# The third block's four engines: instruction order by sort keys, replaced by an order written out step by step

## The reference, cut to what matters

```python
def hybrid_layer(x, norm_gain, w_in, ...):
    hn = rms_norm_3(x, norm_gain)
    proj = jnp.einsum('btd,de->bte', hn, w_in)      # 30 column groups of 128, and 4 forget columns
    log_f = jax.nn.log_sigmoid((ff + b_forget).astype(jnp.float32)).transpose(0, 2, 1)
    o_fox = forgetting_attention(rms_norm_3(fq), rms_norm_3(fk), fv, log_f)
    o_moba = moba_attention(rms_norm_3(mq), rms_norm_3(mk), mv, rel_bias...)
    o_sb = stick_breaking_attention(sq, sk, sv)     # no softmax: logs, a scan, an exponential
    o_swa = swa_sink_attention(rms_norm_3(wq), rms_norm_3(wk), wv, sinks, rel_bias...)
    y = concatenate([o_fox * silu(fg), o_moba * silu(mg), o_sb * silu(sg), o_swa * silu(wg)])
    return x + jnp.einsum('bte,ed->btd', y, w_out)
```

## Time and profile before

| what | value |
|---|---|
| median of 3 runs | 3691.18 us (3691.16 to 3693.05) |
| the profiled execution | 3688.29 us, its span 3686.5 us |
| PE busy in the span | 3161.8 us (86%) |
| DVE busy, ACT busy | 2409.5 us (65%), 1398.1 us (38%) |
| third block | from about 3157 us of the span to its end |

### The profile page before, as it was taken

The page is one execution under the profiler, slowest core; times in us unless marked ns, Lnnn a source line. Parts: engine busy times, 40 slices in busy tenths (PEclk is TensorE's granted clock), DMA queues, the critical chain, the costliest instruction groups (busy, mean ns, idle before and its releaser), DMA issues. The chain is left out here.

```text
span 3686.5 us, 34649 instructions
## 1 busy us (share of the span) xinstructions
PE 3161.8 (86%) x11816; PEld 2026.5 (55%) x11816; DVE 2409.5 (65%) x4718; ACT 1398.1 (38%) x2337; POOL 698.0 (19%) x583
## 2 busy tenths in 40 slices
PE   8988799987887787777788999985999999498878
PEld 4655544433333333333366877764788888465556
DVE  4876456676776777677476445654788888644444
ACT  2324312222222222222253333432788888534442
POOL 0000023344444444444200000000122221000000
PEclk9998799999899999998998999997999999799888
DMA  8322189999999999999821222234899999421101
GB/s 278 113 86 82 40 306 393 404 404 421 417 419 415 415 414 416 420 410 413 317 75 52 78 69 72 86 109 185 291 370 379 372 366 372 147 58 46 29 29 58
DMA packets 351924, 905.63 MB, mean 246 GB/s; under 512 B 29953, under 2 KB 170753, under 8 KB 285570
## 3 DMA queue, kind: packets, MB, share of 16 engines
q0 software_dynamic: 84000, 549.52, 36.4%
q1 hardware_dynamic: 267746, 353.85, 28.1%
HBM read 896.45 MB, written 31.99 MB: 252 GB/s over the span
## 5 line engine op out<-in xcount | busy, mean ns | idle before, releaser
L258 PE MATMUL peer_acc<-peer_uv,peer_diag 128*128 128x512 f32 x2048 | 998.3, 640 | 235.5 <-ACT peer_diag L314 232.5
L435 DVE CUSTOM_DVE_ANT_0 peer_uv<-peer_uv,firsts_h 128x1024 f32<-128x1024 f32 x512 | 627.6, 1227 | 347.2 <-DMA peer_uv<-in_peer_uv,peer_experts 345.7
L258 PEld LDWEIGHTS peer_acc<-peer_uv,peer_diag 128*128 128x128 f32 x2048 | 408.7, 204 | 806.6 <-issue 487.3
L210 POOL DMA_INDIRECT peer_uv<-in_peer_uv,peer_experts x512 | 574.0, 1121 | 1225.0 <-PE peer_acc L258 714.9
L3056 DVE TENSOR_TENSOR slotted_low<-slotted_raw,slotted_high 128x2048 fp32r<-128x2048 f32 x192 | 434.1, 2288 | 66.8 <-ACT slotted_high L3005 66.8
L3005 ACT ACTIVATE slotted_high<-slotted_raw 128x2048 fp32r<-128x2048 f32 x192 | 365.5, 1920 | 64.4 <-PE slotted_h L2962 51.8
L314 ACT ACTIVATE peer_diag<-all_consts,peer_weights 128x128 f32<-128x128 f32 x512 | 166.0, 391 | 329.2 <-DVE peer_weights L428 300.8
L305 ACT ACTIVATE peer_act_in<-peer_act_in 128x4 f32<-128x4 f32 (+1 forms) x130 | 26.6, 205 | 612.2 <-DVE peer_act_in L435 612.2
L2962 PE MATMUL slotted_h<-slotted_high,slotted_xT_high 128*128 128x512 f32 x512 | 205.3, 401 | 6.2 <-DVE slotted_low L3056 4.1
L2962 PE MATMUL slotted_h<-slotted_high,slotted_xT_low 128*128 128x512 f32 x512 | 201.8, 394 | 0.0
L2962 PE MATMUL slotted_h<-slotted_low,slotted_xT_high 128*128 128x512 f32 x512 | 201.8, 394 | 0.0
(11 more groups left out here) (751 smaller groups left out, 5766.5 us busy)
## 6 DMA issues: line engine op xcount, KB each, us to landing
slotted_raw<-in_moe_w SPq DMA_DIRECT2D x192, 1024.0 KB, 8.4
mixers_raw<-in_w_in SPq DMA_DIRECT2D x56, 512.0 KB, 3.7
firsts_ada_raw<-in_w_ada SPq DMA_DIRECT2D x64, 256.0 KB, 2.7
third_raw<-in_w_in SPq DMA_DIRECT2D x30, 512.0 KB, 3.6
firsts_raw<-in_w_in SPq DMA_DIRECT2D x28, 512.0 KB, 4.4
firsts_ada_first<-in_w_ada SPq DMA_DIRECT2D x8, 1024.0 KB, 13.3
peer_uv<-in_peer_uv,peer_experts POOLq DMA_INDIRECT x512, 10.9
ffn_w_raw<-in_peer_wq SPq DMA_DIRECT2D x10, 512.0 KB, 21.9
```

The source lines that it names most:

```text
L210: pool.indirect_dma_start(uv[:, n % R, :, :].rearrange("p a d -> p (a d)"), None, A["peer_uv"], bass.IndirectOffsetOnAxis(ap=experts[:, si ...
L258: mm = nc.tensor.matmul(acc[t % 2][j][:, :], diag[:, n % 4, :], uv[:, n % R, 1, j * BANK:(j + 1) * BANK], start=(m == 0), stop=(m == E - 1))
L435: nc.vector.tensor_tensor_reduce(uv[:, n % R, 0, :], uv[:, n % R, 0, :], h2[:, t, :], 1.0, 0.0, ALU.mult, ALU.add, act_in[:, side, i:i + 1 ...
```

## The change: what it does

Nothing is computed otherwise, and no buffer, bank or semaphore is added or removed. Four things are changed in how the lists are written.

1. `weave` is replaced in the third block by `weave_by`. It takes a string in which each letter names a generator (a is the first argument, b the second, and so on) and a number says how often it goes on. The due times no longer play a part between generators.
2. The generators of the softmax works sort their own steps with a spacing of 2.9 for all kinds. With it the list of each engine has S of work n+1 ahead of T of work n throughout. Before, this was so for moba and swa only, while in fox a work ended (M) before the next began (S).
3. Pieces can be interrupted after every 3 matmuls of the input product (one k), not only after 12. The closing product has such places after every 3 as well, and the string does not use them.
4. On DVE the five operations of a stick head can be interrupted in three places.

```diff
+def weave_by(order, *programs):
+
+    for program in programs:
+        next(program, None)
+    for part in order.split():
+        for _ in range(int(part[1:] or 1)):
+            next(programs[ord(part[0]) - ord("a")], None)
+    assert all(next(program, None) is None for program in programs)
...
                     for k in range(KD):
-                        if k == 4:
-                            yield (starts[p] + ends[p]) / 2
+                        if k:
+                            yield starts[p] + (ends[p] - starts[p]) * k / KD
...
             for n in range(n_works):
-                later += [(work_key[n], 0, n), (work_key[n] + 3.0, 1, n), (work_key[n] + 5.0, 2, n)]
+                at = 2.9 * n
+                later += [(at, 0, n), (at + 3.0, 1, n), (at + 5.0, 2, n)]
...
                     chain(nc.vector.scalar_tensor_tensor(s, z, 0.0, l, ALU.max, ALU.add))
+                    yield sb_key(q) + 6.0 + 2.5 * i
...
             def _(pe):
-                weave(rows_tensor(pe), products(pe), spare_tensor(pe), soft_tensor(pe), stick_tensor(pe))
+                weave_by(THIRD_ORDER["tensor"], rows_tensor(pe), products(pe), spare_tensor(pe), soft_tensor(pe), stick_tensor(pe))
...
+THIRD_ORDER = {
...
+    "tensor": (
+        "a8 b9 c b8 c b8 c b8 c b2 c5 b d2 b6 c b8 c5 b5 c b d b d b5 d2 b d b d2 b d b d2 b2 d b d2 b d b d2 b d "
```

More of the change, by code:

```diff
@@ L3507, in products @@
                         for kk in range(2):
+                            if t or kk:
+                                yield starts[p] + (ends[p] - starts[p]) * (2 * t + kk) / KD
                             k = 2 * kp + kk
@@ L3908, in soft_scalar @@
             for n in range(n_works):
-                later += [(work_key[n] + 2.0, 0, n), (work_key[n] + 4.0, 1, n)]
+                at = 2.9 * n
+                later += [(at + 2.0, 0, n), (at + 4.0, 1, n)]
             for key, what, n in sorted(later):
@@ L3926, in soft_vector @@
             for n in range(n_works):
-                later += [(work_key[n] + 1.0, 0, n), (work_key[n] + 6.0, 1, n)]
+                at = 2.9 * n
+                later += [(at + 1.0, 0, n), (at + 6.0, 1, n)]
             for key, what, n in sorted(later):
@@ L4057, in _ @@
             def _(sp_queue):
-                weave(weights_in(sp_queue), loads(sp_queue), rows_out(sp_queue))
+                weave_by(THIRD_ORDER["sync"], weights_in(sp_queue), loads(sp_queue), rows_out(sp_queue))
                 sp_queue.wait_ge(stored, 16 * 2 * NT)
@@ L4062, in _ @@
             def _(pe):
-                weave(rows_tensor(pe), products(pe), spare_tensor(pe), soft_tensor(pe), stick_tensor(pe))
+                weave_by(THIRD_ORDER["tensor"], rows_tensor(pe), products(pe), spare_tensor(pe), soft_tensor(pe), stick_tensor(pe))
             @block.scalar
             def _(act):
-                weave(rows_scalar(act), rounded(act), emptied_by_scalar(act), gates_opened(act), spare_scalar(act),
+                weave_by(THIRD_ORDER["scalar"], rows_scalar(act), rounded(act), emptied_by_scalar(act), gates_opened(act), spare_scalar(act),
                       forget_scalar(act), soft_scalar(act), stick_scalar(act))
@@ L4071, in _ @@
             def _(dve):
-                weave(rows_vector(dve), rests(dve), spare_vector(dve), forget_vector(dve), soft_vector(dve),
+                weave_by(THIRD_ORDER["vector"], rows_vector(dve), rests(dve), spare_vector(dve), forget_vector(dve), soft_vector(dve),
                       stick_vector(dve), rows_closed(dve))
+THIRD_ORDER = {
+    "sync": (
+        "b a3 b a35 c a c7 "),
+    "tensor": (
[6 rows of a table added]
+    "scalar": (
[4 rows of a table added]
+    "vector": (
[4 rows of a table added]
+}
 def constants():
```

## The result

The changed kernel takes **3645.98 us** (median of 4 runs, 3644.53 to 3647.78), beside 3691.17 us of the kernel before in the same session: ratio 0.9878, 95% interval 0.9861 to 0.9896. It is faster by 1.2%. The profiled execution took 3647.78 us, its span is 3646.0 us.

A forecast was written before the change was run, and what follows sets the result against it. PE bounds the middle stage, held up by the fixed order of steps. Work 325, idle 32 and clock 18 make 375 us instead of 419.3, 44 less, so 3646 us as a median; 8-in-10 range 3621 to 3674.

The forecast's parts named there:

- work of PE: Middle stage, PE at full clock: 319 us stay, +1 for a spreading moved in, +5 for changes of kind, together 325.
- place B: Fox norms: PE idle for the reciprocal with six fewer matmuls in front, and at the third spreading; 3.4 us, before 1.
- fox works: E of work 10 1.5 us late behind logarithms and a table load, two more steps late by 0.6; 3 us idle.
- third stick pair: Stick pair of 384 keys: too little PE work covers its activations and DVE operations; short by 3.8 us.
- stick products: Stick products following their transposes at once, 0.3 to 0.6 us in each of 6 pairs, and a turning; 2.5 us.
- place C: Swa norms: PE idle while ACT loads tables, takes the root, stick exponentials and E of work 23; 4.7 us.
- last gate piece: Spreading starts 6.2 us after emptying starts, released by row sums on DVE behind silu and yT; 6.2 us idle.
- small misses: Waits the count does not see, each engine's queue a little late; 4 us, where before some 8.
- clock: Middle stage: time lost to the low clock level, taken as 18 us (bounds 8 and 40) instead of 40 before.
- the 100 us: Middle stage of 419.3 us: the part that is PE idle time and low clock, from which the gain must come.
- the rival of half the gain: Two open works make ACT and DVE queues collide, idle grows by 24 us; 3670 to 3680 us, chance 0.12.
- The clock rival: Many small PE waits raise the low-clock share above 45% (granted clock 0.77 or less), cancelling the gain or slower; chance 0.05.

The follow-up runs named there:

- m_run12: Changed kernel with its written order, but piece matmuls gathered into runs of at least 12: 3673.74 us, ratio 0.9953 to the kernel before.
- x_pipe: Kernel before with only the fox works overlapped, S of the next work ahead of T, by due times: 3689.42 us, ratio 0.9992.
- x_fine: Kernel before with only pieces made interruptible after every 3 matmuls, order still by due times: 3677.02 us, ratio 0.9955.
- c_after: The changed kernel run again unaltered, as companion of later runs: 3647.56 us, ratio 0.9865 to the kernel before.

## Why the prediction was right, point by point

The time came out on the forecast, 3645.98 for 3646, faster as said. The mechanism held in the main, and two terms were mis-sized in opposite directions.

| term of the middle stage | forecast us | measured us |
|---|---|---|
| work of PE | 325 | 323 to 324 |
| place B | 3.4 | 3.0 |
| fox works | 3 | 0.9 |
| third stick pair | 3.8 | 3.3 |
| moba norms | 2.2 | 2.8 |
| stick products | 2.5 | 1.3 |
| place C | 4.7 | 3.9 |
| swa | 2.5 | 1.5 |
| last gate piece | 6.2 | 6.2 |
| small misses | 4 | 0.7 |
| clock | 18 | 23 to 25 |
| sum | 375 | 372.0 |

- **Where the 100 us lay** was right. m_run12 confirms one half of the mechanism, three matmuls that cover C and W. Of the other half it shows that the written order covers E. But the prediction put this down to PE's pattern, and moba and swa had S ahead of T before, with 23.9 us of waits. At the longest of these ACT's own list held E back, and the share of the written lists of ACT and DVE in the gain wasn't measured. x_pipe and x_fine show that neither S ahead of T in fox nor finer places bring it alone.
- **Work of PE**: 6 us more were expected (1 of spreading, 5 of changes of kind), some 4 came. The price goes with the runs, 0.06 and 0.17 us each in the two series. What makes the difference between these two was not measured.
- **Idle time**: 32 expected, 23.6 measured. The long waits were found one by one within 0.8 us. (At place B the row 3257.38 of the earlier trace rows is a weight load. The multiply, L3792, begins at the same time.) What was too large were the allowances for steps that are a little late: fox, swa, stick products and small misses were put at 12 us and took 4.4. The slack of 0.1 to 0.8 us in the pattern was enough, and the rival of half the gain fell with it.
- **Clock**: 18 expected, some 24 measured, and this step failed in its reasoning. I took less than in proportion to the idle time, since most waits would become short and the long ones few. In fact low clock lay at the few long ones, at four places (B and C, the third stick pair with the moba norms, the last gate piece) 51 us in all. The loss was 0.66 us per us of idle time before and about 1.0 after.
- **Place C and the table loads**: root to load, load to exponential follow one another without a gap, 3472.06 to 3472.09 and 3473.37 to 3473.38 in the rows above. The Trainium skill, ScalarE: Activation LUTs, section What ACT_TABLE_LOAD costs, adds a drain of some 1.38 us. The trace disagrees: the wait is 3.90 us, beside the 7.5 us that the drain would have given.
- **The clock rival** had its mechanism right, though not here: in m_run12, 13 waits below 0.7 us in 55 us went with a granted clock of 0.88. The Trainium skill, TensorE: Matmul & The Clock Gate, section A second HAM failure mode, tells of such micro-idles; by this, the trace agrees. In the changed kernel the three-matmul runs fill these waits, and its clock there is 1.00. The sum of this rival was wrong. The 44 us of gain already hold 22 from the clock, so by the prediction's own terms (325 and 32 us, 0.45 us for each us of low clock) the gain would be gone at a granted clock of about 0.84, and at 0.77 the time would lie some 30 us above that of before.
- **Closing stage**: no change was expected, and it is 2.4 us shorter (49.8 to 47.4). Its idle time is 3.2 us in both. PE's busy time fell by 2.4: one spreading less, as said, and 0.5 us of low clock instead of 2.3. The late rest of the third piece did not show.
- **The sum of both** is some 50 us in the third block (from the first piece matmul to the end 469.1 and 419.4 us), where 44 were forecast. That the median is met to the microsecond is luck in part. The prediction's own terms give 3644 + 2.9, or 3647 us, and the terms of the stage missed by 8 to 9 us of idle time and 6 of clock in opposite directions. And the first two blocks were 9 us longer in the profiled execution. Beside c_after the medians differ by 49.4 us instead of 45.2.
- **What would show it**: PE busy near 350 (348.4), T's and M's waits (4.5 and 1.1 where 10 and 3 were said), and the run of 42 piece matmuls at the end were met. PE waits once for third_low within the stage, for 0.2 us. The clock of 0.94 was missed by 0.01.

## What to carry to other kernels

Where the engine that bounds waits for a chain of short operations in a fixed order, write out the order of the steps on all engines, with the next item's first step ahead of this item's second, and look at what stands ahead of the awaited step in the helping engine's list. That step order alone, in one kind of works and with the rest by due times, brought nothing clear here. Then fill the short gaps that are left with the smallest interruptible pieces of independent work, but only where a gap is: every cut has a price, here 0.06 to 0.17 us. Then look at the single long waits of TensorE. Mending three of those here gave back 1.7 to 3 times what the idle time fell by, as low clock went with them. And compare the stage that was changed, not only the median, when unchanged code before it drifts by more than the effect.

## What the runs showed of the hardware that was not expected

- One wait of 2.33 us at place B was followed by 13.7 us at the low clock level, though PE was busy for 12.5 of them. With the wait at 0.97 us and piece matmuls among the small ones the level stayed high. At place C 3.90 us went with 13.7 to 17.1 us of it, and with two waits of 1.2 and 0.8 us in its place 3.4 us were left.
- With many waits below 0.7 us the clock was lower as well (0.88 at 6.3 us idle in 55), while at 1.0 us idle in 55 it was 1.00. Yet before, 6.8 us idle in 60, most of them in waits of over 1 us, went with 1.00.
- A wait of 3.36 us ahead of large matmuls was followed by no low clock in two executions and by 3.4 us in a third. And in before 3.4 us of low clock began in a row of small products with no wait in the 20 us ahead of it.
- The start of the third block's pieces moved by up to 12.8 us (3217.4 to 3230.2) between executions whose first two blocks are the same instructions. Its cause was not looked for by an experiment and stays open.
